# A two-layer decoder trunk on one core: the first routing round is scored apart, the weights of later heads and the steps of each stage are spread over the slots, and two of eight channel blocks of a convolution move to TensorE

## What is computed

```python
for layer in range(2):
    hn = rms_norm(h, norm_mix[layer])
    h = h + (attention(hn) if layer == 0 else conv(hn))   # attention: 8 MLA + 8 MoBA heads, causal
    h = h + peer(rms_norm(h, norm_ffn[layer]))
out = rms_norm(h, norm_final)

# peer, for 8 heads:
q = (x @ w_q).reshape(T, 8, 2, 128)
s = einsum('thcd,hcnd->thcn', q, subkeys)       # 2 x 128 scores for each token and head
# the best 16 of each half, then the best 16 of the 16 x 16 sums -> idx, g = softmax
act = gelu(einsum('td,thkd->thk', x, u_tab[idx]))
y   = einsum('thk,thkd->td', g * act, v_tab[idx])

# conv: u = a * sigmoid(gate) of one projection, then 31 causal taps per channel,
# layer norm, silu, output projection
```

## Time and profile before

| | us |
|---|---|
| runs shown | 1718.05, 1709.69, 1718.81 |
| the profiled execution, its own time | 1713.54 |
| its span | 1711.7 |
| DVE, PE busy | 1141.1, 1012.3 |
| ACT, POOL busy | 619.2, 611.8 |
| start of slot 0, 128, 256, 384 on DVE | 186.1, 611.5, 989.4, 1372.8 |
| start of the last slot on DVE | 1699.2 |

### The profile page before, as it was taken

The page is one execution under the profiler, slowest core; times in us unless marked ns, Lnnn a source line. Parts: engine busy times, 40 slices in busy tenths (PEclk is TensorE's granted clock), DMA queues, the critical chain, the costliest instruction groups (busy, mean ns, idle before and its releaser), DMA issues.

```text
span 1711.7 us, 19895 instructions
## 1 busy us (share of the span) xinstructions
PE 1012.3 (59%) x6242; PEld 465.1 (27%) x6242; DVE 1141.1 (67%) x3162; ACT 619.2 (36%) x1699; POOL 611.8 (36%) x516
## 2 busy tenths in 40 slices
PE   6987576667447556665476656655356944544443
PEld 3554422222125313332023423332013611101000
DVE  3331376767463478999965468998786566666764
ACT  1312235655123334434233334433142533323221
POOL 0001044434322344545532245554232354444441
PEclk9999775656658758766578868766568965555555
DMA  9104599999999999999998999999997899999996
GB/s 391 45 25 153 218 411 409 336 344 356 414 419 333 352 419 418 401 391 378 401 400 317 358 377 419 407 390 384 420 415 307 325 387 419 419 420 419 419 419 270
DMA packets 90825, 612.24 MB, mean 358 GB/s; under 512 B 10592, under 2 KB 14176, under 8 KB 22112
## 3 DMA queue, kind: packets, MB, share of 16 engines
q0 software_dynamic: 73728, 536.90, 78.3%
q1 hardware_dynamic: 16992, 74.08, 11.4%
HBM read 609.89 MB, written 1.05 MB: 357 GB/s over the span
## 4 chain that ended last, share of the span: by engine, by line
DVE 30%; DMA 29%; PE 23%; issue 9%; ACT 8%; POOL 0%; SPq 0%; DVEq 0%; POOLq 0%; ACTq 0%
DMA ring<-table_dram,idx 21%; DVE ring L1292 13%; PE bank L432 8%; PE qpsum L432 6%; DMA head<-heads_dram 6%; DVE arena L1180 6%; PE ypsum L432 5%; ACT L787 3%; PE bank L437 1%; PE spsum L432 1%; ACT wts L787 1%; DMA arena<-c_out_dram 1%; ACT gel L787 1%; ACT arena L787 1%; DVE topi L1226 1%
## 5 line engine op out<-in xcount | busy, mean ns | idle before, releaser
L425 POOL DMA_INDIRECT ring<-table_dram,idx x512 | 611.6, 1195 | 1074.5 <-PE ypsum L432 748.1
L432 PE MATMUL ypsum<-ring,wts 128*32 128x256 f32 x4096 | 466.3, 546 | 598.5 <-ACT wts L787 594.8
L1292 DVE CUSTOM_DVE_ANT_0 ring<-xns,ring 128x1024 f32<-128x1024 f32 x512 | 621.4, 1223 | 241.5 <-DMA ring<-table_dram,idx 228.1
L787 ACT ACTIVATE gel<-dot 128x1 f32<-128x1 f32 x512 | 103.0, 201 | 742.4 <-DVE dot L1292 721.9
L432 PEld LDWEIGHTS ypsum<-ring,wts 128*32 128x32 f32 x4096 | 98.6, 130 | 928.4 <-ACT wts L787 874.0
L787 ACT ACT_TABLE_LOAD x132 | 169.4, 1283 | 14.9 <-PE bank L437 12.6
L787 ACT ACTIVATE wts<-gident,gel 128x32 f32<-128x32 f32 x512 | 164.6, 321 | 17.2 <-PE ypsum L432 0.2
L432 PE MATMUL qpsum<-head,hT 128*128 128x256 f32 x400 | 118.9, 460 | 49.4 <-DMA head<-heads_dram 48.4
L1180 DVE SCALAR_TENSOR_TENSOR arena<-arena,cols 128x128 f32<-128x128 f32 x480 | 138.8, 349 | 1.0
L432 PEld LDWEIGHTS qpsum<-head,hT 128*128 128x128 f32 x400 | 90.9, 234 | 75.3 <-issue 54.0
L432 PE MATMUL bank<-hT,arena 128*128 128x128 f32 x512 | 87.3, 340 | 0.0
(11 more groups left out here) (139 smaller groups left out, 949.9 us busy)
## 6 DMA issues: line engine op xcount, KB each, us to landing
head<-heads_dram SPq DMA_DIRECT2D x50, 512.0 KB
ring<-w_in_dram SPq DMA_DIRECT2D x4, 2048.0 KB, 16.0
ring<-table_dram,idx POOLq DMA_INDIRECT x512
arena<-c_in_dram SPq DMA_DIRECT2D x4, 2048.0 KB, 20.4
arena<-heads_dram SPq DMA_DIRECT2D x7, 1152.0 KB
arena<-c_out_dram SPq DMA_DIRECT2D x6, 1024.0 KB, 9.5
arena<-w_out_dram SPq DMA_DIRECT2D x1, 4096.0 KB, 36.8
head<-heads_dram SPq DMA_DIRECT2D x25, 128.0 KB
```

What stands on the lines that cost most here:

```text
L425: pool.indirect_dma_start(out=row(b), out_offset=None, in_=table[:, :], in_offset=bass.IndirectOffsetOnAxis(ap=idx[R % 2][:, k:k + 1], axi ...
L432: return nc.tensor.matmul(o_, l, r, start=start, stop=stop, **kw)
L787: return nc.scalar.activation(out_, in_, func, **kw)
L1292: V.tensor_tensor_reduce(out=u, in0=xnr[G % 2], in1=u, scale=1.0, scalar=0.0, op0=ALU.mult, op1=ALU.add, accum_out=dot[:, k:k + 1]).then_i ...
```

## The change

Five things change together.

1. **Start.** The seven constants come through ACT's DMA queue, beside SP's. The input is transposed as it is; its norm (`rnorm`) is applied when ACT takes the projections out of PSUM, and the first projection chunk stands before the turn of the second half.
2. **First round.** The weights and keys of heads 0 to 3 are loaded ahead, into parts of `head`, the attention's buffers and the ring (4 times 1152 KB, 4.72 MB, more to load in all). `early_heads` scores tokens 0 to 31 of these four heads side by side, 32 columns each. Routing of round 0 waits for that alone. Then come chunks 1 and 3, heads 4 to 7 for all 128 tokens, and slot 0. Heads 0 to 3 for the other 96 tokens stand in slots 1 to 19 and are loaded a second time.
3. **Heads and steps.** Heads of later phases stand every 4 slots in place of every 2, the last of them in the next phase's first slots. Steps stand two slots behind the engine before.
4. **Attention in phase 0.** Two heads share a step; a pair stands every 7 slots, in slots 22 to 78, with 8 pairs of exponentials in place of 16 single ones.
5. **Convolution.** Blocks 6 and 7 go to PE: ACT writes a diagonal of a tap's weights (`tap_diagonal`), PE multiplies it with the shifted block (`tap`), 62 of each a phase. DVE keeps 186 taps, three blocks in turn, in slots 21 to 77, each waiting for the last but two. The sigmoid becomes 0.5 tanh(x / 2) + 0.5.

```diff
+DVE_TAPS = [(c, k) for three in ((0, 1, 2), (3, 4, 5)) for k in range(TAPS) for c in three]
+PE_TAPS = [(c, k) for c in (6, 7) for k in range(TAPS)]
+PAIR_SLOT = [22 + 7 * q for q in range(PAIRS)]
-HEAD_SLOT = 25
-GLU_SLOTS = [8, 12, 20, 26, 36, 44, 54, 62]
-TAPS_FROM, TAPS_TO = 17, 90
-NORM_SLOT = [94, 104, 104]
+GLU_SLOT = [6 + 4 * i for i in range(KD)]
+TAPS_FROM, TAPS_TO = 21, 78
+PE_TAPS_FROM, PE_TAPS_TO = 29, 75
+NORM_SLOT = [90, 95, 95]
...
-    return NORM_SLOT[p - 1] + 3 + 2 * h
+    return NORM_SLOT[p - 1] + 3 + 4 * h
...
+            def early_heads():
+                bank = bank_of(pe, EARLY_Q)
+                pe.wait_ge(early_in, 16 * QUAD * (KD // 2 + 1))
+                for k in range(KD):
+                    for s in range(QUAD):
+                        last = mm(bank[s * QT:(s + 1) * QT, 0:2 * HALF], xnT[:, k, 0:QT],
+                                  early_q[s][k // 2][:, k % 2 * 2 * HALF:(k % 2 + 1) * 2 * HALF],
...
+                for c in range(2):
+                    for s in range(QUAD):
+                        last = mm(bank[s * QT:(s + 1) * QT, c * KEYS:(c + 1) * KEYS], q_T[:, c * P + s * QT:...],
...
+            def tap(t, i):
...
+                pe.wait_ge(tap_ready, t * len(PE_TAPS) + i + 1)
+                last = mm(bank[...], diag[i % DIAGS], uT[:, c, k + t * P:k + (t + 1) * P],
+                          k == 0, k == TAPS - 1)
+                last.then_inc(tap_used if i < len(PE_TAPS) - 1 else bank_full[bank_no(TAPS_JOB[t])], 1)
...
+            def tap_diagonal(t, i):
+                c, k = PE_TAPS[i]
+                if i >= DIAGS:
+                    act.wait_ge(tap_used, t * (len(PE_TAPS) - 1) + i - DIAGS + 1)
+                at_ = C_TAPS + c * TAPS + k
+                run(diag[i % DIAGS], ident[:, :], scale=cols[:, at_:at_ + 1]).then_inc(tap_ready, 1)
...
-                run(sig[c % 2], banks[bank_no(j)][:, P:2 * P], ACT.Sigmoid,
-                    bias=cols[:, C_BIN + KD + c:C_BIN + KD + c + 1]).then_inc(sig_ready, 1)
+                own.then(run(sig[i % 2], banks[bank_no(j)][:, P:2 * P], ACT.Tanh, scale=0.5,
+                             bias=cols[:, C_BIN + KD + c:C_BIN + KD + c + 1]))
+                run(sig[i % 2], sig[i % 2], scale=0.5, bias=0.5).then_inc(sig_ready, 1)
...
+            def heads_at(H, a):          # on ACT; on PE a is 4, 2 and 0
+                if a == 6:
+                    head_scores(H)
+                if a == 4:
+                    head_turn(H)
+                if a == 2:
...
+                    head_queries(H)
```

More of the change, by code:

```diff
@@ L66 @@
 J_OT = J_HEAD + 3 * ATTN_HEADS
-J_W = J_OT + 2
+PAIRS = ATTN_HEADS // 2
+J_OT2 = J_HEAD + 3 * PAIRS
+J_W = J_OT2 + 2
 N_MIX = J_W + 2
@@ L223, in build @@
         sig = [v[:, i * P:(i + 1) * P] for i in range(2)]
+        diag = [v[:, (2 + i) * P:(3 + i) * P] for i in range(DIAGS)]
         qq = sb("qq", 4 * P)
@@ L249, in build @@
         posf = sb("posf", TILES)
+        rnorm = sb("rnorm", TILES)
         rows, rinv = part["sums"][:, 0:ATTN_HEADS], part["sums"][:, ATTN_HEADS:2 * ATTN_HEADS]
         nmax = small[:, 14:16]
+        W2 = 2 * 2 * HALF
+        early_q = [[head[:, i * W2:(i + 1) * W2] for i in range(KD // 2)],
+                   [part["qT"][:, 0:W2], part["qT"][:, W2:2 * W2], vmla[1][:, 0:W2], proj[1][:, CHUNK:2 * CHUNK]],
+                   [row(6)[:, i * W2:(i + 1) * W2] for i in range(KD // 2)],
+                   [ring[:, RING * 2 * D + i * W2:RING * 2 * D + (i + 1) * W2] for i in range(KD // 2)]]
+        early_keys = [head[:, HEAD_K:HEAD_W], gident[:, 0:2 * KEYS], proj[1][:, 3 * CHUNK:3 * CHUNK + 2 * KEYS],
+                      proj[1][:, 3 * CHUNK + 2 * KEYS:4 * CHUNK]]
         ypsum = ctx.enter_context(nc.psum_tensor("ypsum", [P, D], f32))
@@ L379, in load_conv_bias @@
                 sp.dma_start(cbias, c_bout[0:1, :].to_broadcast([P, D])).then_inc(cbias_in, 16)
-            load_head(0)
+            for i in range(KD // 2):
+                load_early(0, i)
+            for s in range(QUAD):
+                load_early_keys(s)
+            full(sp, PROJ_JOB[1][0])
+            for s in (2, 3):
+                for i in range(KD // 2):
+                    load_early(s, i)
             full(sp, PROJ_JOB[1][4])
             load_gain(0)
-            for H in range(1, HEADS + 1):
+            full(sp, MIX_AT[0] + J_HEAD + 3 * (HEADS - 1))
+            for i in range(KD // 2):
+                load_early(1, i)
+            for H in range(HEADS + 1):
                 load_head(H)
@@ L591, in beside_attention @@
             def beside_attention(s):
-                if s == 4:
+                for h in range(QUAD, HEADS):
+                    heads_at(h, s - rest_slot(0, h))
+                if s == 3:
                     latents(1)
@@ L933, in head_scores @@
                 full(act, j)
-                for g in range(GROUPS):
+                for g in range(p == 0 and hq == 0, GROUPS):
                     last = run(scores_of(g * PER_GROUP + hq, slice(i * QT, (i + 1) * QT)), banks[bank_no(j)][g * QT:(g + 1) * QT, 0:2 * KEYS])
@@ L1178, in tap @@
                     return
-                own.wait(1)
+                own.wait(2)
                 own.did(V.scalar_tensor_tensor(
```

463 lines of the change are left out of this document (280 added, 183 removed).

## The result

The changed kernel takes 1609.76 us, the median of four runs (1609.41 to 1610.32), beside 1717.78 for the kernel before on the same chip (1709.69 to 1718.81): a ratio of 0.938, with an interval from 0.935 to 0.941. The forecast was 1640, in a range of 1594 to 1684. The profiled execution took 1609.41 us, its span 1607.6, 104.1 less than before.

What follows compares the result with a forecast made beforehand. The prediction took the DMA rate of 420 GB/s as the loop's floor, with losses before the gathers flow and in slower stretches. Its terms summed to -77.8 us, giving 1640 us, whole range 1594 to 1684.

Steps and rivals of the forecast that it cites:

- The forecast's case: Whole kernel: all terms together give 1640 us, own range 1608 to 1672; chance 0.62.
- start: Before the first query matmul: input behind no constants, no norm first, first chunk sooner, so PE starts 9 us earlier.
- first round: First query matmul to PE at slot 0: 89.0 us becomes 66.0, -23.0, with four heads left for later.
- loaded twice, slots 0 to 20: First slots: 4.72 MB loaded again costs +11.2 us, and PE's extra head work beside them shows +5.
- attention: Slots 32 to 79, phase 0: fewer table loads and wider steps win back 16 of 23.7 us lost.
- slots 96 to 127, three phases: Later phases' heads: four slots each let loads arrive, winning back two thirds of 56.9 us, -38.
- convolution: Both convolution stretches: taps moved to PE and an earlier end win back 8 of 24.2 us lost.
- The slower rival: Convolution: taps and diagonals on PE and ACT join the slot's chain, 90.5 us, about 1793; chance 0.06.
- The "end" of my range: Attention in phase 0: the largest gain allowed, all 23.7 us of lost time won back.
- One sign I had named: After slot 96: PE's wait for heads' weights under 5 us in each of the three phases.
- the sign that I had named for being wrong: Convolution: the forecast is wrong if PE's waits for ACT come from the diagonals.
- All waits go: Rival for the whole loop: it runs at 420 GB/s throughout, -131.6 us, 1586; chance 0.13.

Runs made afterwards that it cites:

- cols_first: The changed kernel with the channel constants issued on SP's queue right behind the first input tile, in place of ACT's queue: 1605.4 us, 0.936.
- tables4: The changed kernel with a one-column gelu between a pair's exponentials (16 table loads back) and an early two-column ACT copy at the start: 1610.68 us, 0.940.
- taps_dve: The changed kernel with all 248 taps of a phase on DVE in the same 57 slots, no diagonals or taps on PE: 1632.68 us, 0.952.
- tight_pairs: The changed kernel with the steps of an attention pair one slot behind each other, still a pair every 7 slots: 1617.05 us, 0.944.
- attention3: The changed kernel with attention steps one slot apart, four table loads a pair, the early ACT copy, and a pair every 6 slots: 1644.51 us, 0.959.
- spacing2: The changed kernel with heads of later phases every 2 slots again and their steps one slot apart: 1638.23 us, 0.955.
- steps1: The changed kernel with a head's steps one slot behind the engine before, heads still every 4 slots: 1609.14 us, 0.939.
- few_taps: The changed kernel without DVE's taps from the third on, 174 of 186 a phase, so it computes something else: 1605.6 us, 0.936.

## Why the prediction was right, and by how much its terms were off

The forecast's case held, 30 us above the median that came: all terms have the sign they were given. Each measured number below is from the rows of before and after, in us of the span.

| term | forecast | measured | |
|---|---|---|---|
| start | -9 | -3.1 | first query matmul 117.59, now 114.50 |
| first round | -23.0 | -26.9 | 89.0, now 62.1 |
| loaded twice, slots 0 to 20 | +16.2 | about +12.2 | 4.77 MB more on the page (11.4 at 420 GB/s), and 0.9 of lost rate (176.61 to 264.4, against 206.6 to 286.2) |
| attention | -16 | -23.4 | lost 23.7, now 0.3 |
| slots 96 to 127, three phases | -38 | -49.0 | lost 56.9, now 7.9 |
| convolution | -8 | -11.4 | lost 24.2, now 12.8 |
| sum | -77.8 | -101.6 | -104.1 in all |

Heads, attention and convolution are given by lost rate, as forecast; in time the stretches moved otherwise, as the bytes did. The attention's is 18.6 us shorter and the 16 slots behind it 7.6, and the two of the convolution are 3.8 and 1.2 us longer, with 3.9 and 3 MB more in them. The 2.5 us that the table lacks lie mostly in slots 80 to 95 and in phase 3.

**Start: the mechanism failed.** I had the norm and the weights of the projection bound it. PE's first transpose waited until 10.43 for `cols`, a transfer issued among the first, at 1.18, on ACT's queue, which took 9.21 us beside the input tiles and weights of SP's queue. cols_first shows it: on SP's queue, early, the constants are there at 5.23. The step that I missed is that the kernel's first matmul reads what one more transfer feeds. The projection started at 15.20 in place of 20.74, 5.5 us sooner and not 9. Another 2.2 us went behind it: its 80 pieces took 32.7 us and not 31.4, with 0.9 for the turn of the second half between. tables4 shows one thing more on this path: ACT's first table load, 1.28 us from 11.63 on.

**First round: right, 4 us too small.** Nearly all of its places came: the eighth gather at 182.08 (180 forecast), PE at slot 0 at 176.61 (174), the first gather at 130.66 (127). Each is 2 to 4 us late, less than the 6 us that the start fell short by. The gap of 3.9 us is the early block with its replicated rows (7.5 us, 9.4 forecast) and the chunks, which took 13.90 us, not 15.60. The chunks owe that to the granted clock, which was 1.00 in them now and 0.89 before (window 149.9 to 165.4); no term had it, so this part is luck. Four tiles of 32 columns start together, 0.01 us apart (timeline of PE, the early query matmuls):

```profile
114.50 0.38 PE L497 MATMUL qpsum<-head,hT 128*32 128x256 f32 x1 [0.99 <-ACT hT L920]
114.51 0.40 PE L497 MATMUL qpsum<-arena,hT 128*32 128x256 f32 x1
114.52 0.41 PE L497 MATMUL qpsum<-ring,hT 128*32 128x256 f32 x2
114.72 0.38 PE L497 MATMUL qpsum<-head,hT 128*32 128x256 f32 x1
```

The 32 matmuls took 3.69 us by the chain, exactly what eight full ones took the earlier trace rows, and not the 5.1 that I drew from the loop. What I had wrong is the reading of the loop's row, 20 such matmuls in 4.50 us. Below is that row's window before, and that of the 32 now:

```profile
210.10:214.60 4.50, 4.46 (x41) 1.80 (x41) 4.24 (x14) 2.06 (x10) 2.03 (x2) 0.50 0.26 44
```
```profile
114.50:118.20 3.70, 3.66 (x64) 2.36 (x64) 0.00 (x0) 0.00 (x0) 0.00 (x0) 1.00 0.02 4
```

PE had no gap in either, but the granted clock was 0.50 in the first and 1.00 in the second. The five quads of the row took 0.90 us each at 1.2 GHz, the eight now 0.46 each at 2.4 GHz: read at its clock, the row shows a quarter of a full matmul for each. The other figure, 0.16, came from a quad alone, whose 0.64 us runs from its start to its end and is not the distance to a next one: in the rows above a piece lasts 0.38 us and the next on its tile starts 0.21 to 0.24 later. The rule of the Trainium skill, TensorEngine Tiling (Array Packing), Key Properties, that I weighed against the row, held here, with each tile's weights new: the 3.7 us worked out by it was the measured number. The same page's rule that a change of mode drains the engine has no row of its own here either. The slower rival that it spoke for needed 0.13 or 0.63 us a tap on the path; taps_dve shows the move of the taps to gain 22 us; a price of the change alone is not shown.

**Attention: undersized, and its cause shown in part.** The "end" of my range, all 23.7 gone, is what came. I named 20.5 us of table loads as the part that goes, and slots between the engines beside it. tables4 brings the loads back and lengthens the stretch by 5 us; the steps alone, in tight_pairs, by 7; loads, steps and pace together, in attention3, by 25, and the program by 34. So loads and steps, one at a time, make some 10 of the 23 us. That the rest is the pace, or the loads in a tight order, is argued and not shown.

**Heads: right, undersized.** The pace is the larger cause, as I had it: spacing2 gives 27 to 29 of the 49 us back. The rest may lie with edits that no run undid, such as the earlier `NORM_SLOT`; no run shows it. One sign I had named was wrong. I wanted PE's wait for heads' weights under 5 us a phase; in the first two phases it is:

```profile
PE qpsum L497 <- DMA head<-heads_dram: 10.8, 6, 3.1
```
```profile
PE qpsum L497 <- DMA head<-heads_dram: 16.5, 6, 4.3
```

It was 14.5 before, at 363 GB/s; 16.5 now goes with 412. In steps1 the same two waits are 4.8 and 5.9 us, and its time is the same, so these waits cost nothing that can be seen. None is over 4.3 us, and the ring holds seven slots of 2.5; that the ring is what covers them is my reading. The two slots between steps, which I had counted to this term, are worth nothing (steps1).

**Convolution: the gain came, most of its signs did not.** 2.5 to 2.65 us a slot was named; over the 96 slots it is 2.72 and 2.92, as 260.9 and 280.6 us also hold the later heads' weights, at 408 and 412 GB/s. DVE is busy 0.89 and 0.83 of them, not over 0.9. A tap cost PE 0.58 us, over the 0.46 at which I had ended, a diagonal ACT 0.36 and not 0.27, and PE's weight loads did wait for the diagonals, 39.3 us in 124 taps, 0.32 each: the sign that I had named for being wrong. It isn't one: few_taps, which keeps every tap and diagonal of PE, runs the stretch at 416. What DVE's taps still cost is 4 to 5 us.

**The rest.** Phase 3 takes 323.4 us from its first slot to its last (1271.7 to 1595.1), 326.4 before; I had asked for 326 again, and the 3 us have no cause that a run shows. "All waits go" at 1586 was nearer to the time than its chance of 0.13 says: of its 110.8 us some 80 came.

## What to carry to other kernels

Where a stream sets the rate and every engine takes its work in order, give each added chain a pace at which its load, its steps and the engine's queue fit between two uses, and count the time lost against the stream's best rate in each stretch. Don't count a busy operation as a gain (table loads, waits for weights) before you know that the buffers don't already cover it: here 20.5 us of loads were worth 4 to 5. And when a run shows no difference in the whole, look at the stretch that was edited: here that stretch was 5 us longer, and a side effect at the start was part of what hid it. Before a row is taken as a price, read the granted clock of its window beside it: the same quad of matmuls took 0.90 us at 0.50 and 0.46 at 1.00. When a stage is made ready early, look for what the stream waits for next: the first gather came 31 us earlier and waited for PE, and with PE free it waited for round 1's scores.

## What the runs showed of the hardware that was not expected

- Four 128 x 32 tiles with different weights run at once: 32 float32 matmuls of 256 columns took 3.69 us at a granted clock of 1.00, the time of eight full ones (3.69 at 1.00); at 0.50, 20 of them took 4.50 us.
- The channel constants, issued at 1.18 on ACT's queue, took 9.21 us while SP's queue moved tiles and weights. Issued on SP's queue ahead of the weights, they were there at 5.23.
- Sixteen more table loads of 1.283 us, 20.5 us in all, made a stretch with ACT busy two thirds of it 5 us longer, and the program no longer.
- The DMA engines moved 419 to 421 GB/s in whole slices, most of it indirect gathers of 8 KB rows (536.90 of 617.01 MB in the whole), and more than 421 in no slice of before or after.
